# A mixture-of-experts kernel: experts ordered by token count on the chip, the two with fewest tokens in 64 slots with rounded part and rest side by side

## The reference

```
logits = h @ w_router                          # (256, 8)
top_vals, top_idx = top_k(logits, 2)
combine = sum(one_hot(top_idx) * softmax(top_vals))
for e in range(8):                             # w_gate, w_up: 1024 x 1408, w_down: 1408 x 1024
    y += combine[:, e:e+1] * ((silu(h @ w_gate[e]) * (h @ w_up[e])) @ w_down[e])
x = x + y
```

## Time and profile before

| what | value |
|---|---|
| median of 3 runs | 1055.9 us (1055.19 to 1056.5) |
| the profiled execution | 1055.26 us, its span 1053.2 us |
| granted TensorE clock | 0.998 of full speed |
| busy in the span | TensorE 99%, its weight loads 81%, VectorE 79%, ScalarE 64%, GpSimd 14% |
| layer 1's experts | 659.57 to 1046.29 us of the span |

### The profile page before, as it was taken

The page is one execution under the profiler, slowest core; times in us unless marked ns, Lnnn a source line. Parts: engine busy times, 40 slices in busy tenths (PEclk is TensorE's granted clock), DMA queues, the critical chain, the costliest instruction groups (busy, mean ns, idle before and its releaser), DMA issues.

```text
span 1053.2 us, 15497 instructions
## 1 busy us (share of the span) xinstructions
PE 1040.3 (99%) x5669; PEld 848.2 (81%) x5669; DVE 835.4 (79%) x1164; ACT 678.7 (64%) x971; POOL 144.8 (14%) x177
## 2 busy tenths in 40 slices
PE   8999999999999999999999999999999999999997
PEld 7988888888888888999887878777777777676775
DVE  6879776988666766687967797898898889889885
ACT  7776746556443534676665555877777777777784
POOL 5004332001100000000613000450101010101011
PEclk9999999999999999999999999999999999999999
DMA  9553544567456546363444548799999999999993
GB/s 285 196 163 113 172 128 158 162 230 272 147 209 230 170 140 195 102 221 120 127 164 142 175 143 290 258 388 343 320 357 391 371 333 389 370 388 366 390 378 100
DMA packets 131282, 252.74 MB, mean 240 GB/s; under 512 B 6606, under 2 KB 56868, under 8 KB 131204
## 3 DMA queue, kind: packets, MB, share of 16 engines
q1 hardware_dynamic: 129444, 245.93, 67.0%
q0 software_dynamic: 1296, 4.20, 1.9%
q10 hardware_dynamic: 464, 1.58, 0.4%
HBM read 247.49 MB, written 4.19 MB: 239 GB/s over the span
## 4 chain that ended last, share of the span: by engine, by line
PE 92%; DVE 5%; ACT 1%; issue 1%; DMA 1%; POOL 0%; SPq 0%; DVEq 0%; POOLq 0%; ACTq 0%
PE PS L826 28%; PE PS L1367 12%; PE PS L1369 12%; PE PS L1368 12%; PE PS L1231 8%; PE PS L1232 4%; PE PS L1178 2%; PE PS L1180 2%; PE PS L1179 2%; PE PS L850 2%; DVE m_lo L2223 2%; PE PS L1038 1%; PE PS L1322 1%; DVE scr L2531 1%; DVE big L2523 1%
## 5 line engine op out<-in xcount | busy, mean ns | idle before, releaser
L517 DVE TENSOR_TENSOR w_lo<-ring,w_hi 128x1536 fp32r<-128x1536 f32 (+1 forms) x190 | 304.5, 1618 | 80.0 <-ACT w_hi L504 79.3
L504 ACT ACTIVATE w_hi<-ring 128x1536 fp32r<-128x1536 f32 (+1 forms) x191 | 260.4, 1369 | 99.3 <-PE PS L1232 47.8
L1667 ACT ACTIVATE m_hi<-ring 128x512 fp32r<-128x512 f32 (+2 forms) x256 | 157.8, 632 | 119.7 <-PE PS L826 117.9
L2223 DVE TENSOR_TENSOR m_lo<-ring,m_hi 128x512 fp32r<-128x512 f32 (+2 forms) x256 | 182.3, 743 | 58.3 <-ACT m_hi L1667 56.3
L826 PE MATMUL PS<-m_hi,h_both 128*128 128x512 f32 (+3 forms) x640 | 178.5, 365 | 0.7 <-DVE m_lo L2223 0.6
L826 PEld LDWEIGHTS PS<-m_hi,h_both 128*128 128x128 f32 x640 | 113.0, 188 | 19.9 <-DVE m_lo L2223 2.5
L1231 PE MATMUL PS<-h_both,w_hi 128*128 128x512 f32 x352 | 124.4, 398 | 0.0
L826 PE MATMUL PS<-m_lo,h_both 128*128 128x512 f32 (+3 forms) x320 | 115.0, 359 | 0.0
L1367 PE MATMUL PS<-w_hi,hTe 128*96 128x512 f32 (+1 forms) x288 | 108.8, 378 | 0.0
L1369 PE MATMUL PS<-w_lo,hTe 128*96 128x512 f32 (+1 forms) x288 | 108.1, 375 | 0.0
L1368 PE MATMUL PS<-w_hi,hTe 128*96 128x512 f32 (+1 forms) x288 | 107.7, 374 | 0.0
(11 more groups left out here) (386 smaller groups left out, 1976.1 us busy)
## 6 DMA issues: line engine op xcount, KB each, us to landing
ring<-in_w_in_dram SPq DMA_DIRECT2D x39, 1024.0 KB, 5.2
ring<-in_w_exp_gate_dram SPq DMA_DIRECT2D x48, 768.0 KB, 8.2
ring<-in_w_exp_up_dram SPq DMA_DIRECT2D x48, 768.0 KB, 8.0
ring<-in_w_exp_down_dram SPq DMA_DIRECT2D x24, 1536.0 KB, 8.9
ring<-in_w_branch_dram SPq DMA_DIRECT2D x12, 1024.0 KB, 5.1
ring<-in_w_ffn_gate_dram SPq DMA_DIRECT2D x12, 768.0 KB, 5.5
ring<-in_w_ffn_up_dram SPq DMA_DIRECT2D x12, 768.0 KB, 5.4
ring<-in_w_ffn_down_dram SPq DMA_DIRECT2D x6, 1536.0 KB, 6.3
```

The lines of the kernel that those rows point to most:

```text
L504: act.activation(split_parts(u, j)[0], ring[:, i % NSLOT, w0:w0 + words], ACT.Copy)\
L517: dve.tensor_tensor(lo, ring[:, (j // 2) % NSLOT, w0:w0 + words], hi.bitcast(F32), SUB).then_inc(sem(f"lo_ready{b}"), 1)
L1667: act.activation(hi, raw, ACT.Copy).then_inc(sem("m_hi_ready"), 1)
L2223: dve.tensor_tensor(lo, raw, hi.bitcast(F32), SUB).then_inc(sem("m_lo_ready"), 1)
```

## The change

Places take the role of experts. Place 0 stays expert 0. The other seven experts are ranked by their number of tokens on VectorE, and places 2 and 5 (`SMALL`) get the two with the fewest; what the router gave (places of tokens, masks, counts) is moved to this order, SyncE reads from `order` which expert's weights each place loads, and the loop over experts on SyncE is written out. Places 2 and 5 have 64 slots. Their tokens lie in `hTs` with 64 hi columns and 64 lo columns side by side, so that one matmul with 128 stationary columns does token hi and token lo by a weight part, and all four products are formed with two streams. The sum then has 128 partitions, of which the lower 64 belong to the lo columns: ScalarE copies the bank (`fold`), and a matmul with a shifted identity adds the lower half to the upper (`folded`), eight times in such an expert. The batches become one expert before the stage, three (places 1 to 3) during place 0, four (4 to 7) during place 3. A second pass is needed if a place has more tokens than slots.

```diff
-CAP = 96
-PASSES = -(-T // CAP)
+CAP, FEW = 96, 64
+SMALL = (2, 5)
+PASSES = -(-T // FEW)
...
+FEW_AFTER = {2: [("fold", 0)], 4: [("folded", 0)], 5: [("fold", 1)], 7: [("folded", 1), ("gu", 0)], 8: [("fold", 2)],
+             9: [("tr", 0)], 10: [("folded", 2)], 11: [("fold", 3)], 13: [("folded", 3), ("gu", 1)],
+             15: [("tr", 1), ("fold", 4)], 16: [("tr", 2), ("folded", 4)], 17: [("fold", 5)],
+             18: [("folded", 5), ("gu", 2)], 20: [("tr", 3)]}
+FOLDS, DOWN_FOLDS = 8, (6, 7)
...
-BATCHES = [(0, 2), (2, 3), (5, 3)]
-BATCH_IN = {1: 1, 3: 2}
-BATCH_AFTER = {j: k for k, j in enumerate((6, 7, 9, 10, 12, 13, 16, 18))}
+BATCHES = [(0, 1), (1, 3), (4, 4)]
+BATCH_IN = {0: 1, 3: 2}
+BATCH_AFTER = {0: {j: k for k, j in enumerate((9, 10, 12, 13, 15, 16, 18, 19))},
+               3: {j: k for k, j in enumerate((6, 7, 9, 10, 12, 13, 16, 18))}}
+PREVIOUS_FOLDED, PREVIOUS_ROWS = 2, 6
+TSLOT = (0, 1, 2, 4, 0, 1, 2, 3)
...
# SyncE
-            with sp.Fori(1, NE) as e:
-                expert_loads(eg, eu, ed, e, e)
+            sp.wait_ge(sem("routing_known"), ROUTING_KNOWN["order_known"])
+            for e in range(1, NE):
+                expert_loads(eg, eu, ed, expert_in(e), e)
...
# TensorE
+            def folded(r, e, i):
+                pe.wait_ge(sem("fold_full"), fold_no(r, e, i) + 1)
+                bank, n = fold_of(i)
+                pe.matmul(PS[:, bank, 0:n], shift[:, :, :], folds[:, i % 2, 0:n], start=False, stop=True,
+                          skip_group_check=True).then_inc(sem("folded"), 1)
...
+                def two(dst, x, whi, wlo, start, stop):
+                    pe.matmul(dst, x, whi, start=start, stop=False)
+                    return pe.matmul(dst, x, wlo, start=False, stop=stop)
...
+                            if e in SMALL:
+                                mm = two(PS[:, 2 * (g % 2) + up, 0:gn * P], hTe_few[:, kt, :, :], hi[:, k, :], lo[:, k, :],
+                                         kt == 0, kt == KD - 1)
+                                continue
...
-                    if e == 0 and j == 3:
+                    if e == 0 and j == 0 and isinstance(r, int):
+                        first_gathered(r, KD // 2)
+                        expert_counts()
+                    if e == 0 and j == 4:
                         row_scales(r)
...
# ScalarE
+            def fold(r, e, n, i):
+                bank, words = fold_of(i)
+                x = fold_no(r, e, i)
+                wait_used(act, expert_unit(n), fold_after(i))
...
+                act.activation(folds[:, i % 2, 0:words], PS[:, bank, 0:words], ACT.Copy).then_inc(sem("fold_full"), 1)
...
# VectorE
+            def sorted_places():
+                dve.wait_ge(sem("totals_full"), 1)
+                dve.wait_ge(sem("constants"), 1 + HALF + 3 + 1)
+                step(dve.tensor_copy(counts, PS[:, LOGIT_BANKS[1], NE:2 * NE]))
+                step(dve.tensor_tensor(key, counts, key_off, ADD))
+                step(dve.tensor_tensor(smaller, key.unsqueeze(1).broadcast_to([P, NE, NE]), key.unsqueeze(2).broadcast_to([P, NE, NE]),
+                                       ALU.is_lt))
+                step(dve.tensor_reduce(size_rank, smaller, AX.X, ADD))
+                step(dve.tensor_tensor(moves, size_rank.unsqueeze(1).broadcast_to([P, NE, NE]),
+                                       rank_at.unsqueeze(2).broadcast_to([P, NE, NE]), ALU.is_equal))
+                step(dve.tensor_tensor(mixed, by_expert.unsqueeze(2).broadcast_to([P, 8, NE, NE]),
+                                       moves.unsqueeze(1).broadcast_to([P, 8, NE, NE]), MUL))
+                step(dve.tensor_reduce(by_place, mixed, AX.X, ADD))
+                dve.tensor_copy(order[:, 1:NE], expert_at[:, 1:NE]).then_inc(sem("routing_known"), 1)
...
                 if isinstance(r, int):
                     for j in range(2, EARLY):
                         rest_lo(dve, (1, 0), j)
+                    sorted_places()
                     most_rows()
```

More of the change, by code:

```diff
@@ L86, in expert_after, with slot_runs, slots_of, fold_no @@
 def expert_after(e, j):
-    what = list(EXPERT_AFTER.get(j, ()))
+    what = list((FEW_AFTER if e in SMALL else EXPERT_AFTER).get(j, ()))
     if e == 0 and j == INFO_AFTER:
         what.append(("info", 0))
-    if e in BATCH_IN and j in BATCH_AFTER:
-        what.append(("gather", BATCH_AFTER[j]))
-    return what
+    if e in BATCH_IN and j in BATCH_AFTER[e]:
+        what.append(("gather", BATCH_AFTER[e][j]))
+    if e - 1 in SMALL and j == PREVIOUS_FOLDED:
+        what.append(("rows_folded", 0))
+    return what
+def slot_runs(batch):
+    e0, ne = BATCHES[batch]
+    runs = []
+    for e in range(e0, e0 + ne):
+        if e not in SMALL and runs and runs[-1][-1] not in SMALL and TSLOT[e] == TSLOT[runs[-1][-1]] + 1:
+            runs[-1].append(e)
+        else:
+            runs.append([e])
+    return runs
+RANK_AT = [0] + [0] * (NE - 1)
+for _i, _e in enumerate(SMALL + tuple(e for e in range(1, NE) if e not in SMALL)):
+    RANK_AT[_e] = _i + 1
+def slots_of(e):
+    return FEW if e in SMALL else CAP
+def fold_no(r, e, i):
+    return FOLDS * (len(SMALL) * r + SMALL.index(e)) + i
 def place_aux():
@@ L249, in hybrid_trunk @@
         ring = sb("ring", [P, NSLOT, SLOT])
+        shift, folds = over(("shift", [P, 2, FEW], F32R), ("folds", [P, 2, 512], F32R))
         x_tok = sb("x_tok", [P, TT, D])
         hT, = over(("hT", [P, KD, T], F32))
+        hTs, = over(("hTs", [P, TSLOTS, 2 * KD * CAP], F32R))
         hTe, w_hi_last = over(("hTe", [P, TSLOTS, 2, KD, CAP], F32R), ("w_hi_last", [P, 1, SLOT // 2], F32R))
@@ L747, in _ @@
                 with sp.Fori(1, npass) as r:
-                    with sp.Fori(0, NE) as e:
-                        expert_loads(eg, eu, ed, e, r * NE + e, again=True)
+                    for e in range(NE):
+                        expert_loads(eg, eu, ed, expert_in(e) if e else 0, r * NE + e, again=True)
         @block.tensor
@@ L1348, in turn, with expert_counts @@
                 mm.then_inc(sem(f"aux_full{b}"), 1)
+            def expert_counts():
+                for a in range(TT):
+                    mm = pe.matmul(totals, ones[:, :], msel[:, a, :], start=(a == 0), stop=(a == TT - 1))
+                mm.then_inc(sem("totals_full"), 1)
+            def folded(r, e, i):
[3 more added lines that the diff above has]
+                          skip_group_check=True).then_inc(sem("folded"), 1)
             def row_scales(r):
@@ L1358, in row_scales @@
                 mm.then_inc(sem("rsl_full"), 1)
-                if isinstance(r, int):
-                    for a in range(TT):
-                        mm = pe.matmul(totals, ones[:, :], msel[:, a, :], start=(a == 0), stop=(a == TT - 1))
-                    mm.then_inc(sem("totals_full"), 1)
             def expert(r, e, n):
@@ L1568, in _ @@
             pool.wait_ge(f, n + 1)
+            for q in range(NE):
+                pool.memset(by_expert[:, 7, q:q + 1], float(q))
+                pool.memset(key_off[:, q:q + 1], q / 16.0 if q else -2.0 * T)
+                pool.memset(rank_at[:, q:q + 1], float(RANK_AT[q]))
+                pool.memset(cap_at[:, q:q + 1], float(slots_of(q)))
+                pool.memset(weight_at[:, q:q + 1], CAP / slots_of(q))
             step(pool.memset(tri, 1.0))
@@ L2689, in tokens @@
                 wait_aux_full(dve, b, uses)
-                s0 = e0 % TSLOTS
-                dve.tensor_copy(hTe[:, s0:s0 + ne, 1, k:k + 1, :],
-                                PS[:, 4 + b, 0:ne * CAP].rearrange("p (k e c) -> p e k c", k=1, e=ne))\
-                   .then_inc(sem(f"aux_free{b}"), 1)
+                runs = slot_runs(batch)
+                for run in runs:
+                    s0, c0, n = TSLOT[run[0]], (run[0] - e0) * CAP, len(run)
+                    if run[0] in SMALL:
+                        ins = dve.tensor_copy(few_tokens(run[0])[:, k, 1, :], PS[:, 4 + b, c0:c0 + FEW])
+                    else:
+                        ins = dve.tensor_copy(hTe[:, s0:s0 + n, 1, k:k + 1, :],
+                                              PS[:, 4 + b, c0:c0 + n * CAP].rearrange("p (k e c) -> p e k c", k=1, e=n))
+                    if run is runs[-1]:
+                        ins.then_inc(sem(f"aux_free{b}"), 1)
             def first_tokens(r, pair):
```

161 lines of the change are left out of this document (114 added, 47 removed).

## The result

| | median | runs |
|---|---|---|
| before, on the same chip | 1055.68 us | 1055.19 to 1056.5, 4 runs |
| after | 1071.03 us | 1067.5 to 1074.04, 4 runs |

The ratio is 1.0143, with an interval of 1.011 to 1.0177: slower by 15.3 us, where 1052.0 was forecast and 1057.5 was the upper end. The profiled execution took 1067.5 us, its span is 1065.8.

What follows compares the result with a forecast made beforehand. TensorE bounds at 46.86 us an expert, DMA within a microsecond and leading once TensorE shortens. Terms 3.3 + 1.0 - 3.8 + 0.7 - 5.1 = -3.9 us give 1051.4 profiled, median 1052.0; range 1046.5 to 1057.5.

Steps and rivals of the forecast that it cites:

- The bound: Per expert: TensorE at 46.86 us, DMA within a microsecond of it and leading once TensorE gets shorter.
- The sort, +3.3: Start of expert 0: sorting on VectorE delays piece 4, 3.3 us in all, bounds +1.3 to +5.
- Rival A: More room: clock not lost, sort hidden, weights moved 2% faster in both stretches; about 1047 us, chance 0.19.
- The clock behind it, +1.0: After TensorE's 3.6 us idle stretch before piece 4, matmuls at 1.2 GHz cost 1.0 us, bounds 0 and 3.
- Gathers moved, 0: Gathers moving from expert 1 to place 0: +4.2 us in place 0, -4.2 in place 1, net 0.
- the prediction's own sign: Stated sign of being wrong: expert 0 ends other than 3 to 5 us late, after allowing 4.2 for gathers.
- Four at once in place 3, +0.7: Place 3: gathering four experts, 384 columns for 288; only the four gathers after D0 count, 0.7 us.
- Place 2, -3.8: Two streams for three in place 2: lead 3.1 us, row addition 0.7, reserve 0; together 3.8 us gained.
- place 5, -5.1: Two streams for three in place 5: lead 3.4 us, rows 0.7, reserve 1.0; together 5.1 us gained.
- rival C: Places 2 and 5: ScalarE's queue waits for TensorE, slots release late, DMA idles, gains go; 1060.9 us, chance 0.12.
- The lead: TensorE's slack over landed weights at D0 of places 3 and 6, used up to some 3.3 us after landing.
- Rival D: Small places: TensorE at 1.2 GHz throughout, 40 us more in all, 1092 us; chance 0.02 shared with another rival.

Runs made afterwards that it cites:

- (13): Changed kernel with ScalarE's and VectorE's steps in the small places three pieces behind TensorE's order, not four: 1064.7 us.
- (6): Kernel with place 1 kept as expert 1 and the sort behind the logit gap, with its small places removed: 1057.66 us.
- (14): The best kernel, but one expert gathered ahead, three in place 0 behind pieces 6 to 18, four in place 3: 1057.36 us.
- (3): Changed kernel with no small places, all keeping 96 slots and three streams; sort, order and gathers stay: 1069.38 us.
- the best kernel: Changed kernel with place 1 kept, sort behind the logit gap, lag of three in small places, no zero matmuls: 1051.56 us, ratio 0.9963 to before.
- (8): Changed kernel plus only 27 matmuls against zeros in TensorE's waits in places 2 and 5: 1069.4 us.

## Why the prediction was wrong

Two steps failed: the cost of place 0 (8.5 us more forecast with its gathers, 16.0 measured) and the gain of the small places (8.9 forecast, 2.4 measured). With 1.1 too little for place 3 and 0.5 for place 6 they are 15.6 of the 16.1 us by which the profiled execution missed its forecast of 1051.4. The median lies another 3.5 above that execution, where the forecast had 0.6. That goes with the clock: from the shortest to the longest the four executions have mean clocks of 0.990, 0.989, 0.984 and 0.986, and 0.0035 of 1070 us, from the profiled one to the middle of the four, is 3.7.

**The bound.** That DMA is close behind TensorE and takes the lead in a small place was right: the DMA share there is 1.02 to 1.04 and ScalarE waits for landings. TensorE is busy 37.7 and 37.3 us, where 33.4 was forecast; in (13), at full clock, it is 36.4 and 36.6.

**The sort, +3.3.** Right. Piece 4 starts at 671.53 (671.1 forecast) after 3.38 us of idleness (3.6). Well placed, it leaves 2.1 us (6), where 1.3 was the lower bound. (Rival A takes 1.3 off for a hidden sort; by that bound it would be 2.0.)

**The clock behind it, +1.0.** The mechanism was right, the size wrong: 6.8 us at 1.2 GHz, all of them with work, 3.4 us. The seven slow matmuls that I counted were a number of my own choice.

**Gathers moved, 0.** Wrong, and with the clock it makes place 0's miss of 7.5 us. I took the 4.2 of the earlier trace rows as a price that moves along, and it is the price in place 1. Place 0 has `pall`, counts, row information and late weights in the same queues; that these make the difference is the likely reading, which no run separates. The gathers behind pieces 15 to 19 also shared banks with transposes just made: 3.8 us in two waits. In (14), without these and at full clock, they still cost 6.9. For place 0 of after that is 4.2 + 3.3 + 3.4 + 3.8 = 14.7 of the 16.0 measured; the rest isn't resolved. By the prediction's own sign, expert 0 ends 11.8 us late after allowing 4.2, and not 3 to 5.

**Four at once in place 3, +0.7.** Mis-sized: 52.98 - 51.14 = 1.84. The row of (3), four experts and no small places, has 52.50, so 1.4 of it is the gathers, the price of all eight (8 x 0.18): the four ahead of D0 were not hidden in a wait for weights, because in after TensorE reaches D0 8.3 us behind its landing. The other half microsecond is two folds of place 2's rows (x256 matmuls for x254), which fall into place 3. Place 6 takes 47.31 and not 46.86 for the same reason, and the sum had nothing for it.

**Place 2, -3.8, and place 5, -5.1.** 0.0 and -2.4. The step that failed is the sentence against rival C, that each such step comes four pieces after its work, 8 us of landing. This is the cause itself: in a place bound by landings, a step of the queue four pieces behind stands behind landings that TensorE has not needed yet. TensorE's waits of about 2 us are then followed by the lower clock, which makes its work longer just where it is late. It isn't rival C as written: the DMA share stays above 1. That place 2 takes its 46.9 all the same is a coincidence. With a lag of three the places win 2.4 and 5.3 (with place 1 kept), 2.4 and 3.8 in the changed kernel; by medians, the best kernel (1051.56) is 6.1 us below the one without small places (1057.66), of 8.9 forecast. The lead is used up, as forecast, but already at D0 of places 2 and 5 themselves: there the first matmul stands 3.8 us behind the landing in after, 3.4 and 3.7 in the best kernel, where I said 3.3 for D0 of places 3 and 6 (8.3 and 6.2 in after). So the gain was there at the middle of the place, and was lost in its second half, where three of the four transposes are.

**Rival D** was dismissed by a sum over the whole place (it costs only beyond 26 us at the lower level). The clock costs wherever TensorE's work is the next to end: 6.83 us at the lower level held 4.94 of work, so 2.5 us. And the earlier trace rows, 10 us at full clock with 7.32 busy, said little about waits of 2 to 3 us in one piece. The Trainium skill, TensorE: Matmul & The Clock Gate, section HAM oscillation — how this bites in real kernels, has a kernel whose matmuls wait in each tile and pay with their clock; by that rule the traces agree, since the clock fell in places 2 and 5 of all six profiled kernels that had small places with unfilled waits at a lag of four (3.4 to 10.2 us in each place). The waits here, 1.8 to 3.6 us, are mostly shorter than that kernel's.

**What adds up.** From after, in medians: place 1 kept -8.7, sort moved -4.4, lag of three -6.4, in all 1071.0 to 1051.6. It is near the time forecast, 1052.0, but reached by three edits that the change did not have, so it doesn't bear the forecast out.

**Open.** Why the clock fell at 657 to 659 in five of the eight profiled executions in which a single expert is gathered ahead, and in none of nine (before among them) in which it is two (one of those fell at 649): TensorE's busy share there is nearly the same, 4.8 and 4.7 of 5 us, and none of these six falls has a wait of even 0.5 us between 640 and it. And why place 5 takes 41.5 us with place 1 kept and 43.1 without, at a like lead.

## What to carry to other kernels

When an edit shortens one engine's work so that transfers become the bound, look at every step that another engine does a fixed number of pieces later: that distance was chosen for a busy TensorE, and is now counted in landings. Price a moved step at the place where it arrives, by the queues and banks that are busy there, not by what it cost where it was. And price, with each wait of TensorE of about 2 us, a lower clock behind it: half of TensorE's busy time in the stretch that follows, which was 1.6 to 3.4 us in after. A few matmuls on zeros in the waits show whether the clock is part of the loss; read it from the windows of the stage, since medians of four runs didn't settle it in (8).
